# State-space scan with the output products of two heads issued together, one in each half of the array's columns, and a fourth decay matrix

## The chip, the cores and the metric

The kernel runs on one core of a Trainium2 chip, as one launch. The metric is the device time of that core in microseconds (us). TensorE is written PE in the profile (PEld its weight loads), VectorE DVE, ScalarE ACT, and SP the queue that issues the DMAs.

## The reference

The program computes, in float32, a two-layer transformer block on 256 tokens and 256 context tokens and then, on 16 + 256 tokens, one layer that joins a state-space scan with a short convolution and ends in a mixture of experts. The change lies in the scan. Its core in the reference is this, for 16 heads of 64 channels in 4 groups, in chunks of 128 tokens:

```python
seg = A_cum[..., :, None] - A_cum[..., None, :]
Lmat = jnp.exp(jnp.where(causal, seg, -jnp.inf)).astype(dtype)
CB = jnp.einsum('bcqgn,bckgn->bcgqk', Cc, Bc)
y_diag = jnp.einsum('bcgqk,bcgrqk,bckgrp->bcqgrp', CB, Lmat, xdt)
...
y_off = jnp.einsum('bcqgn,bcgrpn,bcgrq->bcqgrp', Cc, prev, decay_out)
return (y_diag + y_off).reshape(b, Lp, SSD_HEADS, SSD_HEADDIM)
```

## The kernel before

The kernel holds activations with features on the partitions and tokens along the free axis (272 here: a chunk of 16, two of 128). It does not carry a state from chunk to chunk. For each head it builds the whole causal matrix of decay times C.B over all pairs of chunks, and multiplies it with the head's inputs. The matrix of a head is 656 columns wide in SBUF: columns 0 to 272 belong to the 16 source tokens of the first chunk and use 16 partitions, 272 to 528 to the second chunk's 128 source tokens, 528 to 656 to the third's. It is called `EE`, and before the change there are three of them, used in turn by h % 3.

The work of a head h is spread over three engines:

- TensorE broadcasts the running sums of the decays (`pe_head_decay`, L2154, three float32 products, six instructions in the trace, since the trace shows two for each float32 product).
- VectorE adds a bias and clips (L2184 to L2186), ScalarE takes six exponentials (L2167 to L2173), VectorE multiplies with C.B (L2190, L2191).
- TensorE forms the output (`pe_head_out`, L2201, L2202, L2203): 64 channels of `XD` times the matrix, in three products of 272, 256 and 128 columns that add up in one PSUM bank. An even head writes partitions 0 to 63 of the bank, an odd one 64 to 127, so two heads share a bank. After the odd head VectorE adds the skip term and gates (L2216, L2219).

The scan is interleaved with a projection, the second half of `win`: 24 output tiles of 24 float32r matmuls each (L486 to L488 in `mm3`, three matmuls for a product, since both operands are held as a high and a low part). The weights of two tiles arrive in one DMA, ScalarE makes the high part (L461), VectorE the low part (L471). After tile f TensorE runs step f - 1 of the scan (`pe_scan`); VectorE and ScalarE run the same steps in their own programs. Step f = 5 + i does the decay part of head i and the output part of head i - 2. The short convolution lies between them: every third step VectorE computes a tile of it (L2027 to L2039), ScalarE squares it (L2017), and TensorE adds the sums of its squares (`pe_sc_sum`, L2046, 16 columns of the array). After every odd head from the second pair on, TensorE adds the squares of the pair before (L2230, 4 columns).

At step 22 stands `pe_sc_norm` for six convolution tiles. A spread (L2068) brings the inverse root of a tile's two groups to 64 partitions each, two products of 272 columns with 16 rows in the two halves of the array's columns. VectorE scales the tile (L2081), ScalarE copies its high part (L2076), VectorE subtracts the low part (L2084). The outputs of head 15 stand behind these spreads on TensorE. Then follows the output projection `wout`. In its first block of 36 matmuls each k waits for a tile's low part, and behind the block stand the last sum L2046 and the spreads of the last two tiles, which wait for a second square root (L2055, ScalarE) and reciprocal (L2060, VectorE). That reciprocal is called the second inverse below.

What sets the order are the programs of the engines, written out by hand. Each engine executes in order, and waits for counted marks of the others (`at`, `up`). PSUM has eight banks, handed out in turn: `bank` waits until the bank that was given back longest ago is free.

The program has other matmuls that use only some of the array's columns. L533 multiplies a modulation weight block with 32 columns, four products of 512 columns in the four 32-column strips, each with all 128 rows and another block of weights as moving data.

## Time and profile before

| | before |
|---|---|
| runs, us | 1783.9 median of three (1780.74 to 1784.62) |
| the profiled execution's own time | 1783.91 us |
| its span | 1782.1 us |
| PE busy | 1695.4 us (95%) |
| PEld busy | 1358.6 us (76%) |
| DVE busy | 1034.1 us (58%) |
| ACT busy | 832.7 us (47%) |
| mean granted TensorE clock | 0.977 of full |
| chain that ended last | PE 85%, DVE 7%, ACT 4% |

The profile is of one execution. Its span goes from the first to the last instruction, its own time also holds the start and the end. Busy time of an engine is the union of its instructions' times. The chain that ended last is followed back from the last instruction, at each step to what released it. A timeline row gives start, duration, engine, line and form, and in brackets how long the engine had been idle and what ended it. The clock is the share that the chip granted TensorE, 1.00 being 2.4 GHz and 0.50 being 1.2 GHz.

### The profile page before, as it was taken

How to read it: one execution, taken by the hardware profiler on the slowest of the kernel's cores; microseconds unless marked ns; L12 is line 12 of the kernel's file. 1: busy time of each engine (PE TensorE's matmuls, PEld its weight loads, DVE VectorE, ACT ScalarE, POOL GpSimd, SP SyncE). 2: the span in 40 equal slices, each digit the busy share in tenths (PEclk: the TensorE clock that was granted, in tenths of full speed). 3: DMA queues.
4: the chain of work that ended last, by engine and by line, in shares of the span. 5: the costliest groups of instructions: out<-in, count | busy, mean ns of one | idle time of the engine just before them, and what ended most of it. 6: DMA issues, size and time to landing. Idle time of an engine off the chain costs nothing.

```text
span 1782.1 us, 25094 instructions
## 1 busy us (share of the span) xinstructions
PE 1695.4 (95%) x10390; PEld 1358.6 (76%) x10390; DVE 1034.1 (58%) x1497; ACT 832.7 (47%) x1194; POOL 0.9 (0%) x5
## 2 busy tenths in 40 slices
PE   5989989999999999998898999999999999999996
PEld 2745667777877787898588999899876968777875
DVE  2235655544334444535756566647666558888885
ACT  3334552633223322523746454554444347766764
POOL 0000000000000000000000000000000000000000
PEclk7999999999999999999999999999998999999998
DMA  9311533344334424233024454344222419989982
GB/s 375 112 52 67 202 112 120 116 154 164 130 124 175 178 78 170 87 115 119 1 72 142 163 204 160 118 167 160 95 95 71 142 45 380 339 334 342 353 329 99
DMA packets 42678, 287.76 MB, mean 161 GB/s; under 512 B 4784, under 2 KB 5936, under 8 KB 11200
## 3 DMA queue, kind: packets, MB, share of 16 engines
q1 hardware_dynamic: 42384, 285.97, 44.0%
q8 instruction: 85, 1.39, 0.3%
q14 instruction: 33, 0.27, 0.0%
q10 hardware_dynamic: 144, 0.06, 0.0%
q0 software_dynamic: 32, 0.07, 0.0%
HBM read 285.03 MB, written 1.05 MB: 161 GB/s over the span
## 4 chain that ended last, share of the span: by engine, by line
PE 85%; DVE 7%; ACT 4%; issue 2%; DMA 1%; DVEq 0%; SPq 0%; ACTq 0%
PE ps L486 17%; PE ps L487 16%; PE ps L488 16%; PE ps L2670 5%; DVE WL L471 3%; PE ps L2640 2%; PE ps L2644 2%; PE ps L533 2%; PE ps L2641 2%; PE ps L1356 1%; PE ps L1454 1%; PE ps L1425 1%; DMA ring<-wts 1%; PE ps L511 1%; PE ps L613 1%
## 5 line engine op out<-in xcount | busy, mean ns | idle before, releaser
L486 PE MATMUL ps<-HH,WH 128*128 128x512 f32 (+2 forms) x1488 | 495.8, 333 | 17.4 <-DVE WL L471 10.2
L471 DVE TENSOR_TENSOR WL<-ring,WH 128x2048 fp32r<-128x2048 f32 (+2 forms) x191 | 413.5, 2171 | 164.4 <-ACT WH L461 164.1
L488 PE MATMUL ps<-HH,WL 128*128 128x512 f32 (+2 forms) x1488 | 484.8, 326 | 0.0
L487 PE MATMUL ps<-HL,WH 128*128 128x512 f32 (+2 forms) x1488 | 484.2, 325 | 0.0
L461 ACT ACTIVATE WH<-ring 128x2048 fp32r<-128x2048 f32 (+2 forms) x191 | 346.7, 1817 | 206.4 <-DMA ring<-wts 77.9
L486 PEld LDWEIGHTS ps<-HH,WH 128*128 128x128 f32 x1488 | 284.8, 191 | 68.3 <-issue 32.7
L488 PEld LDWEIGHTS ps<-HH,WL 128*128 128x128 f32 x1488 | 284.9, 191 | 21.8
L487 PEld LDWEIGHTS ps<-HL,WH 128*128 128x128 f32 x1488 | 285.4, 192 | 20.8 <-issue 0.5
L486 PE MATMUL ps<-parts,WH 128*128 128x512 f32 (+1 forms) x352 | 119.7, 340 | 0.0
L487 PE MATMUL ps<-parts,WH 128*128 128x512 f32 (+1 forms) x352 | 118.4, 336 | 0.0
L488 PE MATMUL ps<-parts,WL 128*128 128x512 f32 (+1 forms) x352 | 118.3, 336 | 0.0
L2640 PE MATMUL ps<-WH,HH 128*128 128x512 f32 x256 | 102.4, 400 | 6.6 <-DVE WL L471 6.6
L829 DVE SCALAR_TENSOR_TENSOR X<-ps,modv,X 128x256 f32<-128x256 f32 x72 | 32.4, 481 | 124.5 <-PE ps L488 124.5
L2644 PE MATMUL ps<-WH,HL 128*128 128x512 f32 x256 | 100.0, 391 | 0.0
L2641 PE MATMUL ps<-WL,HH 128*128 128x512 f32 x256 | 99.8, 390 | 0.0
L471 DVE TENSOR_TENSOR WL<-arena,WH 128x2048 fp32r<-128x2048 f32 x38 | 86.4, 2287 | 3.9 <-ACT WH L461 3.7
L461 ACT ACTIVATE WH<-arena 128x2048 fp32r<-128x2048 f32 x38 | 72.8, 1919 | 31.4 <-PE ps L2644 17.2
L2670 PE MATMUL ps<-WH,parts 128*128 128x512 f32 x256 | 72.9, 396 | 2.7 <-DVE parts L2751 1.5
L486 PEld LDWEIGHTS ps<-parts,WH 128*128 128x128 f32 x352 | 66.8, 190 | 9.0 <-issue 1.8
L488 PEld LDWEIGHTS ps<-parts,WL 128*128 128x128 f32 x352 | 66.8, 190 | 6.9
L487 PEld LDWEIGHTS ps<-parts,WH 128*128 128x128 f32 x352 | 66.8, 190 | 6.6
L533 PE MATMUL ps<-ring,scond 128*32 128x512 f32 x384 | 55.7, 659 | 14.5 <-DMA ring<-wts 8.1
(350 smaller groups left out, 2213.9 us busy)
## 6 DMA issues: line engine op xcount, KB each, us to landing
ring<-wts SPq DMA_DIRECT2D x206, 1024.0 KB, 5.0
arena<-wts SPq DMA_DIRECT2D x38, 1024.0 KB, 6.5
ring<-wts SPq DMA_DIRECT2D x32, 704.0 KB, 4.1
X<-xin SPq DMA_DIRECT2D x4, 512.0 KB, 9.2
cst<-csts SPq DMA_DIRECT2D x1, 1373.0 KB, 15.3
ring<-wts SPq DMA_DIRECT2D x3, 384.0 KB, 2.9
out<-arena SPq DMA_DIRECT2D x2, 512.0 KB, 2.9
ring<-wts SPq DMA_DIRECT2D x1, 640.0 KB, 3.5
```

What stands on the lines that cost most here:

```text
L461: e.activation(split_parts(i)[0], raw(i), ACT.Copy).then_inc(*up("high", i))
L471: e.tensor_tensor(lo, raw(i), hi.bitcast(F32), ALU.subtract).then_inc(*up("low", i))
L486: e.matmul(o, w[0][:, cols], x[0], start=k == 0, stop=False)
L487: e.matmul(o, w[0][:, cols], x[1], start=False, stop=False)
L488: return e.matmul(o, w[1][:, cols], x[0], start=False, stop=k == nk - 1)
L511: e.matmul(o[1][m], v[0][:, 256 * k + 128 * m:256 * k + 128 * m + 128], at_k(x, k)[h], start=k == h == 0, stop=False)
L533: t = e.matmul(ps[32 * j:32 * j + 32, b, :], scond[:, 2 * k:2 * k + 32], w[:, 512 * j:512 * j + 512], start=k == 0, stop=k == 7)
L829: t = e.scalar_tensor_tensor(out=X[:, j, a:z], in0=B("out", key, j)[:, a:z], scalar=modv[l][:, gt + j, s:s + 1], in1=X[:, j, a:z], op0=ALU ...
L2640: e.matmul(ps[:, b, :], XG[0][:, k, g], w[0][:, s], start=k == 0, stop=False)
L2641: e.matmul(ps[:, b, :], XG[0][:, k, g], w[1][:, s], start=False, stop=False)
L2644: t = e.matmul(ps[:, b, :], XG[1][:, k, g], w[0][:, s], start=False, stop=k == 7)
L2670: t = e.matmul(ps[:, bs[n], :], HTE[p][:, z, hs], w[q][:, s], start=first and p == q == 0, stop=last and p == 1)
```

## The change

`pe_head_out` does nothing for an even head. For an odd head it takes the bank, waits for the decay matrices of both heads of the pair, and issues their six products in alternation: the first chunk's for the even head and for the odd one, then the second chunk's, then the third's. The heads' shapes and numbers are unchanged, and so is the number of products. Since an even head's matrix is now read a step later, there are four matrices in place of three. The fourth lies in `cst` from the table `r128` on, over tables that only the attention stages read. ScalarE and VectorE wait before they write a matrix for the output of head h - 4 in place of h - 3. Lines behind the change move by 2 to 8: L2154 becomes L2156, L2184 to L2186 and L2190, L2191 move by 2, L2068 and L2081 become L2070 and L2083, L2203's successor is L2210 for all three products, L2216 and L2230 become L2224 and L2238.

```diff
--- before.py
+++ after.py
@@ -1793,7 +1793,9 @@
         YP = parts(16, NT)
         top[0] = 0
         ZS, XC, YC, XD = area(8, NT), area(16, NT), area(8, NT), area(3, 1024)
-        CBm, EE = area(4, 656), area(3, 656)
+        CBm, EE3 = area(4, 656), area(3, 656)
+        late = cat["r128"][0]
+        EE = [EE3[:, z, :] for z in range(3)] + [cst[:, late:late + 656]]
         dtr, dab, dtl, dtt, dA, aex = (area(48) for _ in range(6))
         bias6 = area(96)
         spare = XF[:, 8 * NT:]
@@ -2159,55 +2161,61 @@
             return lambda i, n: bias6[0:n, 16 * i + h:16 * i + h + 1]
 
         def act_head_decay(e, h):
-            z, y = h % 3, h % 2
+            EZ, y = EE[h % 4], h % 2
             b, bc = B("head", h), head_bias(h)
             e.wait_ge(*at("head_mixed.near", h))
-            if h >= 3:
-                e.wait_ge(*at("head_out", h - 3))
-            e.activation(EE[0:16, z, 0:16], SG2[0:16, y, 0:16], ACT.Exp).then_inc(*up("head_exp.meta", h))
-            e.activation(EE[0:16, z, 16:144], b[0:16, 16:144], ACT.Exp, bias=bc(3, 16), scale=1.0)
-            e.activation(EE[0:16, z, 144:272], b[0:16, 144:272], ACT.Exp, bias=bc(4, 16), scale=1.0)
-            e.activation(EE[:, z, 400:528], b[:, 144:272], ACT.Exp, bias=bc(5, 128),
+            if h >= 4:
+                e.wait_ge(*at("head_out", h - 4))
+            e.activation(EZ[0:16, 0:16], SG2[0:16, y, 0:16], ACT.Exp).then_inc(*up("head_exp.meta", h))
+            e.activation(EZ[0:16, 16:144], b[0:16, 16:144], ACT.Exp, bias=bc(3, 16), scale=1.0)
+            e.activation(EZ[0:16, 144:272], b[0:16, 144:272], ACT.Exp, bias=bc(4, 16), scale=1.0)
+            e.activation(EZ[:, 400:528], b[:, 144:272], ACT.Exp, bias=bc(5, 128),
                          scale=1.0).then_inc(*up("head_exp.far", h))
-            e.activation(EE[:, z, 272:400], EE[:, z, 272:400], ACT.Exp)
-            e.activation(EE[:, z, 528:656], EE[:, z, 528:656], ACT.Exp).then_inc(*up("head_exp", h))
+            e.activation(EZ[:, 272:400], EZ[:, 272:400], ACT.Exp)
+            e.activation(EZ[:, 528:656], EZ[:, 528:656], ACT.Exp).then_inc(*up("head_exp", h))
 
         def dve_head_decay(e, h):
-            z, y = h % 3, h % 2
+            EZ, y = EE[h % 4], h % 2
             b, bc = B("head", h), head_bias(h)
             e.wait_ge(*at("decay_bias"))
             e.wait_ge(*at("head", h))
             if h >= 2:
                 e.wait_ge(*at("head_exp.meta", h - 2))
-            if h >= 3:
-                e.wait_ge(*at("head_out", h - 3))
+            if h >= 4:
+                e.wait_ge(*at("head_out", h - 4))
             e.tensor_scalar(SG2[0:16, y, 0:16], b[0:16, 0:16], bc(0, 16), 0.0, ALU.add, ALU.min)
-            e.tensor_scalar(EE[:, z, 272:400], b[:, 16:144], bc(1, 128), 0.0, ALU.add, ALU.min)
-            e.tensor_scalar(EE[:, z, 528:656], b[:, 144:272], bc(2, 128), 0.0, ALU.add,
+            e.tensor_scalar(EZ[:, 272:400], b[:, 16:144], bc(1, 128), 0.0, ALU.add, ALU.min)
+            e.tensor_scalar(EZ[:, 528:656], b[:, 144:272], bc(2, 128), 0.0, ALU.add,
                             ALU.min).then_inc(*up("head_mixed.near", h))
             e.wait_ge(*at("head_exp", h))
             e.wait_ge(*at("cb_masked", h // 4, 1))
-            e.tensor_tensor(EE[0:16, z, 0:272], EE[0:16, z, 0:272], CBm[0:16, h // 4, 0:272], ALU.mult)
-            e.tensor_tensor(EE[:, z, 272:656], EE[:, z, 272:656], CBm[:, h // 4, 272:656],
+            e.tensor_tensor(EZ[0:16, 0:272], EZ[0:16, 0:272], CBm[0:16, h // 4, 0:272], ALU.mult)
+            e.tensor_tensor(EZ[:, 272:656], EZ[:, 272:656], CBm[:, h // 4, 272:656],
                             ALU.mult).then_inc(*up("head_mixed", h))
 
         def pe_head_out(e, h):
-            z, r, x = h % 3, 64 * (h % 2), h // 2
-            b = banks.of["y", x] if h % 2 else bank(e, "y", x)
-            hc = slice(64 * h, 64 * h + 64)
-            e.wait_ge(*at("head_mixed", h))
-            if h == 0:
+
+            if h % 2 == 0:
+                return
+            x = h // 2
+            b = bank(e, "y", x)
+            pair = (h - 1, h)
+            for i in pair:
+                e.wait_ge(*at("head_mixed", i))
+            if h == 1:
                 e.wait_ge(*at("xd", 2, 1))
-            e.matmul(ps[r:r + 64, b, 0:272], XD[0:16, 0, hc], EE[0:16, z, 0:272], start=True, stop=False)
-            e.matmul(ps[r:r + 64, b, 16:272], XD[:, 1, hc], EE[:, z, 272:528], start=False, stop=False)
-            e.matmul(ps[r:r + 64, b, 144:272], XD[:, 2, hc], EE[:, z, 528:656], start=False,
-                     stop=True).then_inc(*up("head_out", h))
-            if h % 2:
-                banks.give(b, "y_gated.skip", x)
-                if x == 0:
-                    bank(e, "group_sums")
-                else:
-                    pe_group_sum(e, x - 1)
+            for c, o, a, n in ((0, 0, 0, 272), (1, 16, 272, 256), (2, 144, 528, 128)):
+                for i in pair:
+                    r = 64 * (i % 2)
+                    t = e.matmul(ps[r:r + 64, b, o:o + n], XD[0:TLEN[c], c, 64 * i:64 * i + 64],
+                                 EE[i % 4][0:TLEN[c], a:a + n], start=c == 0, stop=c == 2)
+                    if c == 2:
+                        t.then_inc(*up("head_out", i))
+            banks.give(b, "y_gated.skip", x)
+            if x == 0:
+                bank(e, "group_sums")
+            else:
+                pe_group_sum(e, x - 1)
 
         def dve_head_out(e, h):
             if h % 2:
```

On TensorE, step 9 of the scan before (head 4's broadcasts, head 2's outputs) and the start of the next tile:

```order
L2154 MATMUL ps<-cst,arena 128x16
L2154 MATMUL ps<-cst,arena 128x128 x2
L2201 MATMUL ps<-arena 64x272
L2202 MATMUL ps<-arena 64x256
L2203 MATMUL ps<-arena 64x128
L486 MATMUL ps<-HH,WH 128x272
```

The same step with the change:

```order
L2156 MATMUL ps<-cst,arena 128x16
L2156 MATMUL ps<-cst,arena 128x128 x2
L486 MATMUL ps<-HH,WH 128x272
L487 MATMUL ps<-HL,WH 128x272
L488 MATMUL ps<-HH,WL 128x272
```

Nothing stands between the broadcasts and the tile any more. On TensorE, step 10 before (head 5's broadcasts, head 3's outputs, the sum of the squares of the first pair, a sum of the short convolution):

```order
L2154 MATMUL ps<-cst,arena 128x16
L2154 MATMUL ps<-cst,arena 128x128 x2
L2201 MATMUL ps<-arena 64x272
L2202 MATMUL ps<-arena 64x256
L2203 MATMUL ps<-arena 64x128
L2230 MATMUL ps<-arena,cst 4x272
L2046 MATMUL ps<-X,cst 16x272
```

The same step with the change, where the rows that read `cst` are those of head 3, whose matrix is the fourth:

```order
L2156 MATMUL ps<-cst,arena 128x16
L2156 MATMUL ps<-cst,arena 128x128 x2
L2210 MATMUL ps<-arena 64x272
L2210 MATMUL ps<-cst,arena 64x272
L2210 MATMUL ps<-arena 64x256
L2210 MATMUL ps<-cst,arena 64x256
L2210 MATMUL ps<-arena 64x128
L2210 MATMUL ps<-cst,arena 64x128
L2238 MATMUL ps<-arena,cst 4x272
L2048 MATMUL ps<-X,cst 16x272
```

Head 2's three products have moved here, each ahead of head 3's of the same chunk. The order on the other engines is unchanged.

## Rows read from the trace of the kernel before

**Rows 1.** Windows, head steps: stretch, its us, busy us by engine, clock, DMA, GB/s.

```profile
1260.10:1356.60 96.50, 96.50 (x619) 76.06 (x618) 62.88 (x131) 47.88 (x127) 0.00 (x0) 1.00 0.25 88
```

**Rows 2.** Chain of waits, steps f = 5 to 10; start us, us, what.

```profile
1260.15 0.96 PE ps L2154 x6
...
1264.14 0.96 PE ps L2154 x6
...
1279.82 0.96 PE ps L2154 x6
1280.79 0.60 PE ps L2201 x2
1281.38 0.58 PE ps L2202 x2
1281.96 0.22 PE ps L2203 x2
...
1285.40 0.96 PE ps L2154 x6
```

**Rows 3.** Timeline, TensorE column-tiled products; start us, us, engine, line, form, count, [idle before].

```profile
173.52 0.16 PEld L533 LDWEIGHTS ps<-ring,scond 128*32 128x32 f32 x8 [0.17 <-issue]
173.52 1.06 PE L533 MATMUL ps<-ring,scond 128*32 128x512 f32 x8
...
1360.16 1.11 PE L2201 MATMUL ps<-arena 16*64 16x272 f32 x2
1361.20 1.12 PE L2202 MATMUL ps<-arena 128*64 128x256 f32 x2
...
1374.62 2.08 PE L2068 MATMUL ps<-X,cst 16*64 16x272 f32 x8 [4.02 <-DVE X L2060]
1376.62 1.07 PE L2230 MATMUL ps<-arena,cst 128*4 128x272 f32 x2
```

**Rows 4.** Timeline of VectorE, its waits in the head steps.

```profile
1284.24 0.43 DVE L2190 TENSOR_TENSOR arena<-arena 16x272 f32<-16x272 f32 x1 [1.43 <-ACT arena L2173]
...
1286.46 0.22 DVE L2184 TENSOR_SCALAR X<-ps,arena 16x16 f32<-16x16 f32 x1 [1.32 <-issue]
...
1298.62 0.22 DVE L2184 TENSOR_SCALAR X<-ps,arena 16x16 f32<-16x16 f32 x1 [0.74 <-issue]
...
1310.87 0.22 DVE L2184 TENSOR_SCALAR X<-ps,arena 16x16 f32<-16x16 f32 x1 [0.78 <-PE ps L2154]
...
1322.56 0.22 DVE L2184 TENSOR_SCALAR X<-ps,arena 16x16 f32<-16x16 f32 x1 [2.50 <-issue]
...
1334.71 0.22 DVE L2184 TENSOR_SCALAR X<-ps,arena 16x16 f32<-16x16 f32 x1 [0.73 <-issue]
```

**Rows 5.** Head 12: its last VectorE product, and its output products on TensorE.

```profile
1333.44 0.54 DVE L2191 TENSOR_TENSOR arena<-arena 128x384 f32<-128x384 f32 x1
...
1340.74 0.60 PE ps L2201 x2
```

**Rows 6.** Timeline of VectorE, last weight split, first spread, second inverse.

```profile
1353.75 2.29 DVE L471 TENSOR_TENSOR WL<-ring,WH 128x2048 fp32r<-128x2048 f32 x1
1357.30 0.50 DVE L2081 SCALAR_TENSOR_TENSOR arena<-arena,vec,ps 128x272 f32<-128x272 f32 x1 [1.26 <-PE ps L2068]
...
1372.72 1.84 DVE L2060 RECIPROCAL X<-X 16x272 f32<-16x272 f32 x1 [1.89 <-ACT X L2055]
```

**Rows 7.** Windows: two stretches at the lower TensorE clock, and one after.

```profile
1359.10:1365.80 6.70, 6.48 (x18) 2.94 (x19) 4.22 (x11) 2.15 (x5) 0.00 (x0) 0.50 0.15 64
...
1372.80:1386.20 13.40, 11.58 (x41) 8.15 (x42) 8.94 (x13) 3.67 (x6) 0.00 (x0) 0.50 0.16 65
1386.40:1400.00 13.60, 13.60 (x101) 12.58 (x100) 7.90 (x13) 3.31 (x6) 0.00 (x0) 1.00 0.43 151
```

**Rows 8.** Windows of the stages after the scan.

```profile
1378.00:1440.00 62.00, 61.96 (x461) 54.33 (x461) 35.67 (x51) 21.87 (x28) 0.00 (x0) 0.93 0.29 103
...
1500.00:1560.00 60.00, 58.45 (x269) 47.15 (x268) 49.06 (x30) 42.42 (x32) 0.00 (x0) 1.00 0.90 340
```

## The prediction, made before the changed kernel was run

> **What bounds the kernel now.** I read the windows view over the sixteen head steps first. TensorE is busy for all 96.5 us of it, VectorE for 62.9 and ScalarE for 47.9 [rows 1]. So there each microsecond of TensorE work is on the path of the stage. The chain of waits shows what it holds: per head three broadcast sums (L2154), then the output products of the head two before (L2201, L2202, L2203) at 0.60, 0.58 and 0.22 us, which is 1.40 [rows 2]. A step without output products lasts 1264.14 - 1260.15 = 3.99 us and one with them 1285.40 - 1279.82 = 5.58 [rows 2]. The products therefore cost 1.59 us a step, 0.19 more than their own time: what the array loses when it turns from 128-column tiles to 64-column ones and back.
>
> Second, I read VectorE's timeline for idle time that TensorE ends. Its wait for ScalarE's exponentials, 1.43 us before L2190, belongs to a head's own chain and stays. Five waits before L2184 end with the broadcast sums: 1.32 + 0.74 + 0.78 + 2.50 + 0.73 = 6.07 us [rows 4]. One more comes at the end, 1.26 us before the first spread is used (L2081) [rows 6]. That is 7.33 us in all. This number matters because of what comes behind it. From 1357.30 to 1374.62 the work runs as a ladder on VectorE and ScalarE: six times L2081, L2076 and L2084, then the last gate, the last short-convolution tile, a weight split, a square root with its table load, and the reciprocal L2060 [rows 6]. TensorE waits 4.02 us for that reciprocal [rows 3]. So what reaches the rest of the kernel is not what TensorE saves, but how much earlier VectorE gets to L2081.
>
> **The change, part by part.** *Pairing.* Per pair six products are issued in alternation over the two column halves, where before 2 x 3 were issued in two different steps. Whether two halves run at once is the question. No row has 128 rows on 64-column tiles side by side with different moving data, so I bound it by its neighbours. L533 has 128 rows, four 32-column strips and a different moving block for each: its eight passes over 512 columns take 1.06 us, and all eight weight loads are done in 0.16 [rows 3]. L2068 has 16 rows and two 64-column halves. At the lower clock, two pairs of heads' spreads, eight passes of 272 columns, take 1376.62 - 1374.62 = 2.00 us, 1.00 a pair. At the same clock one single head's L2201, two passes of the same width, takes 1361.20 - 1360.16 = 1.04 [rows 3]. The second half is free there. I take free. The other bound is no overlap at all.
>
> With free overlap a pair costs what one head costs, and the even head's products vanish from its step. There are eight even heads. In five of their steps (heads 2, 4, 8, 10, 14) nothing narrow is left and the full 1.59 goes. In three (0, 6, 12) the 16-column sum L2046 still follows, so the turn of the tile shape stays and 1.40 goes. TensorE's saving is 5 x 1.59 + 3 x 1.40 = **12.1 us**. Without overlap only the turns go, 5 x 0.19 = 1.0 us.
>
> A rule of the Trainium skill speaks against the free half: "TensorE: Matmul & The Clock Gate", Part 3, says that a weight load overlaps a matmul in flight only where the row groups differ. Both halves here use all rows, so by it nothing would overlap and the sum would be the 1.0 us. The trace disagrees: L533's strips share all 128 rows, and its loads still ran within 0.16 us.
>
> *Four decay matrices.* No instruction is added. The fourth lies over constants that only the attention stages read. The wait for head_out(h - 3) becomes one for head_out(h - 4). For an even h that output now leaves TensorE in the same step as output h - 3 did before, for an odd h a step earlier than it did, so VectorE meets no later wait. An even head's matrix is held a step longer, and the fourth matrix covers that. Cost 0.
>
> *Deferred even output.* The pair waits for the odd head's last product, as the odd head did before. Head 12's product was ready at 1333.98, its output started at 1340.74 [rows 5], so 6.8 us of slack lie there. TensorE can come at most 12.1 - 7.3 = 4.8 us closer to VectorE, so no wait comes in its place inside the steps. The y bank is taken a step later, which frees a bank sooner. Cost 0.
>
> *What reaches VectorE.* Before the wait of 1.32 us (head 5) TensorE has saved heads 0 and 2, 2.99 us. Before those of heads 7, 9, 11 and 13 it has saved 4.58, 5.98, 7.57 and 9.16, against 2.06, 2.84, 5.34 and 6.07 of waits to that point [rows 2, 4]. At L2081 it is 12.1 against 7.33. TensorE is ahead each time, so all six waits go and nothing more. The remaining 4.8 us become idle time on TensorE inside the six spreads, because the later ones and the products behind them need PSUM banks that ScalarE and VectorE (L2081) free.
>
> *Behind the scan.* TensorE is 100% and 97% busy in two windows behind [rows 8], and the weight loads follow the splits. I take a pure shift. Before, the clock was at its lower level in two stretches, 1359.1 to 1365.8 and 1372.8 to 1386.2 [rows 7]. Both follow TensorE's thin or missing work around the two spreads, and I take both as they are. Costs: the first dip may last through the first block of the out projection. Busy time there is 13.60 us / 101 matmuls = 0.135 us each at the full clock [rows 7], so its 36 matmuls would lose at most 4.9, less a slack of at most the 4.02 us wait: 0.9 to 4.9 if it happens. The second dip could end earlier. It costs at most half of 1386.2 - 1374.6 = 11.6 us, so 5.8 is the most that could be won and I count 1 to 2 either way.
>
> **The sum.** The profiled execution took 1783.91 us (span 1782.1), and the median of three runs is 1783.9, so nothing is to be corrected between them. 1783.9 - 7.3 = **1776.6 us**, 0.4% faster. About 0.2%, 3.6 us, is what a measurement of this kernel can tell from no change, so "faster" means under 1780.3.
>
> **The rivals.**
> 1. *The clock takes some back.* TensorE will idle longer before the fifth spread, about 4.8 us more. If the first dip covers the block behind it (0.9 to 4.9) and the second ends later (1 to 2), 3.5 us go and the time is 1780.1. For it: the lower clock follows idle stretches here. Against: it came back by 1365.8, soon after dense work began at 1364.8.
> 2. *The whole 12.1 us arrive*, if VectorE can catch up as well: 1771.8. Against: after its six waits VectorE has the 1.43 us waits on ScalarE and its own work, none of which the change touches.
> 3. *The halves run one after the other*, by the page's rule above. TensorE saves 1.0 us and the time is 1782.9: the change would not do what it says.
> 4. *Slower.* The halves do not overlap, and each alternation between them pays the turn of the tile shape. Place: 6 turns in each of 8 pairs, 48. Price: 0.19 us each [rows 2], 9.1 us, less 1.0: +8.1 on a TensorE that bounds the steps, 1792.0. It decides from 0.02 us a turn for any loss, from 0.10 for one over 0.2%. Against: L2068 alternates halves in just this way and pays none [rows 3].
>
> **How the numbers follow.** Forecast 0.74, with 1775 to 1778.5 as its own range. Rival 1 0.10, rival 2 0.05, rival 3 0.07, rival 4 0.04. Faster: the forecast, rival 2 and half of rival 1, which lies at the edge: 0.84. Same: rival 3 and the other half of rival 1: 0.12. Slower: 0.04. The range leaves out rivals 3 and 4 and the far end of rival 2, and goes from 1772.5 (a second dip that ends early, or part of rival 2) to 1780.5 (rival 1).
>
> **What would show it.** In the changed kernel the products at L2210 should start in twos, so that a pair's six take about 1.4 us. An even head's step should be about 4.0 us, the five waits of VectorE before L2184's successor should be gone, and TensorE should wait some 5 us within L2070, the new place of L2068. The second reciprocal should end about 7.3 us earlier, at 1367.2, with the stages behind unchanged in length. It is wrong if a pair takes near 2.8 us (rivals 3 and 4), if L2083 starts over 9 us earlier (rival 2), or if the two stretches at the lower clock change by more than 3 us.

## The result, and the profile after

The changed kernel takes 1774.85 us (median of five runs, 1773.07 to 1776.6), against 1783.3 us (five runs, 1780.74 to 1784.62) for the kernel before on the same chip: a ratio of 0.9958 with a 95% interval of 0.9946 to 0.9969. By the medians that is 8.45 us less, by the ratio 7.5 (5.5 to 9.6), where 7.3 were forecast. The runs don't tell these apart. The profiled execution took 1774.6 us, 9.31 less than the one before.

The page of the changed kernel starts so:

```profile
span 1772.8 us, 25093 instructions
...
PE 1683.5 (95%) x10390; PEld 1351.8 (76%) x10390; DVE 1033.3 (58%) x1497; ACT 833.2 (47%) x1194; POOL 0.9 (0%) x5
```

TensorE is busy 11.9 us less (1695.4 before). VectorE and ScalarE do the work they did.

The windows view of the changed kernel over its head steps, its two stretches at the lower clock and one behind them (columns as in [rows 1]):

```profile
1261.18:1345.64 84.46, 84.46 (x612) 70.68 (x611) 58.36 (x126) 44.55 (x121) 0.00 (x0) 1.00 0.29 100
1350.40:1357.20 6.80, 6.32 (x24) 2.38 (x24) 4.33 (x12) 2.58 (x7) 0.00 (x0) 0.50 0.44 154
1367.50:1374.30 6.80, 6.59 (x23) 3.85 (x24) 4.10 (x8) 1.23 (x3) 0.00 (x0) 0.50 0.08 31
1374.40:1388.00 13.60, 13.60 (x101) 12.59 (x100) 9.36 (x14) 5.35 (x6) 0.00 (x0) 1.00 0.25 83
```

The head steps last 84.5 us instead of 96.5 [rows 1]. The first stretch at the lower clock is as long as before, the second 6.8 us instead of some 13.7 [rows 7]. In the last window the same 101 matmuls fill the same 13.60 us.

TensorE's timeline, changed kernel: an even head's step, a pair's step in the middle of the scan, and the spreads.

```profile
1261.16 1.03 PE L2156 MATMUL ps<-cst,arena 16*128 16x16 f32 x6
...
1321.62 1.03 PE L2156 MATMUL ps<-cst,arena 16*128 16x16 f32 x6
...
1325.60 1.03 PE L2156 MATMUL ps<-cst,arena 16*128 16x16 f32 x6
1326.56 0.44 PE L2210 MATMUL ps<-arena 16*64 16x272 f32 x1
1326.57 0.44 PE L2210 MATMUL ps<-cst,arena 16*64 16x272 f32 x1
1326.84 0.39 PE L2210 MATMUL ps<-arena 16*64 16x272 f32 x1
1326.85 0.39 PE L2210 MATMUL ps<-cst,arena 16*64 16x272 f32 x1
1327.16 0.43 PE L2210 MATMUL ps<-arena 128*64 128x256 f32 x1
1327.17 0.43 PE L2210 MATMUL ps<-cst,arena 128*64 128x256 f32 x1
...
1327.96 0.62 PE L2238 MATMUL ps<-arena,cst 128*4 128x272 f32 x2
...
1337.43 1.48 PE L2210 MATMUL ps<-arena 16*64 16x272 f32 x12
1338.84 0.62 PE L2238 MATMUL ps<-arena,cst 128*4 128x272 f32 x2
...
1345.64 1.59 PE L2070 MATMUL ps<-X,cst 16*64 16x272 f32 x12
1347.86 0.67 PE L2070 MATMUL ps<-X,cst 16*64 16x272 f32 x4 [0.63 <-DVE arena L2224]
1350.88 2.08 PE L2070 MATMUL ps<-X,cst 16*64 16x272 f32 x8 [2.35 <-ACT X L2016]
```

The products start in twos, 10 ns apart, one in each half of the columns. From a pair's first product to the instruction behind its last one it takes 1.40 us (1327.96 - 1326.56), and 1.41 in the other row; one head took 1.40 in the same measure [rows 2]. An even head's step lasts 1325.60 - 1321.62 = 3.98 us. And within the six spreads TensorE, which waited for nothing there before, now waits 0.63 and 2.35 us, for banks that VectorE and ScalarE have to free.

The weight loads of one such pair of products, changed kernel (PEld):

```profile
1327.16 0.13 PEld L2210 LDWEIGHTS ps<-arena 128*64 128x64 f32 x1 [0.41 <-issue]
1327.17 0.13 PEld L2210 LDWEIGHTS ps<-cst,arena 128*64 128x64 f32 x1
1327.21 0.14 PEld L2210 LDWEIGHTS ps<-arena 128*64 128x64 f32 x1
1327.22 0.14 PEld L2210 LDWEIGHTS ps<-cst,arena 128*64 128x64 f32 x1
```

Four loads with all 128 rows start within 0.06 us, while the matmuls that started at 1327.16 and 1327.17 are under way. By themselves they don't show that the halves run at once; the matmuls' own starts do.

VectorE's timeline, changed kernel: head 5, then the last split, the first use of the spread and the second inverse.

```profile
1280.95 2.29 DVE L471 TENSOR_TENSOR WL<-ring,WH 128x2048 fp32r<-128x2048 f32 x1
1283.15 0.22 DVE L2186 TENSOR_SCALAR X<-ps,arena 16x16 f32<-16x16 f32 x1
1286.14 0.22 DVE L2186 TENSOR_SCALAR X<-ps,arena 16x16 f32<-16x16 f32 x1
...
1348.20 2.28 DVE L471 TENSOR_TENSOR WL<-ring,WH 128x2048 fp32r<-128x2048 f32 x1
1350.40 0.49 DVE L2083 SCALAR_TENSOR_TENSOR arena<-arena,vec,ps 128x272 f32<-128x272 f32 x1
...
1365.82 1.84 DVE L2062 RECIPROCAL X<-X 16x272 f32<-16x272 f32 x1 [1.89 <-ACT X L2057]
```

No L2186 has idle time before it, where L2184 had it five times [rows 4], and the 1.26 us before the first use of the spread [rows 6] are gone.

Below, three lengths are read from each trace, since executions start the scan up to 5.4 us apart (1257.2 to 1262.6 us). The **lead** goes from the first broadcast sum to VectorE's first use of the spread. The **ladder** goes from there to the end of the second inverse. The **rest** goes from the start of the second spreads to the end. For the two profiles:

| | before | after | difference |
|---|---|---|---|
| first broadcast sum | 1260.08 | 1261.16 | +1.08 |
| lead | 97.22 | 89.24 | -7.98 |
| ladder (the second spreads start 0.05 us behind it) | 17.27 | 17.26 | -0.01 |
| rest | 407.5 | 405.1 | -2.4 |

These add up to the 9.3 us between the two profiled executions. The first row lies ahead of anything the change touches.

### The profile page after: what moved, and what is told of

Its sections match the earlier page's. It is cut to its first block, busy times and chain, and to the rows that moved or that the text cites. A ratio compares the mean times of both kernels' runs of the same rounds, so it can differ in the third digit from the quotient of the medians.

```text
span 1772.8 us, 25093 instructions
## 1 busy us (share of the span) xinstructions
PE 1683.5 (95%) x10390; PEld 1351.8 (76%) x10390; DVE 1033.3 (58%) x1497; ACT 833.2 (47%) x1194; POOL 0.9 (0%) x5
## 3 DMA queue, kind: packets, MB, share of 16 engines
q8 instruction: 85, 1.39, 0.3%
## 4 chain that ended last, share of the span: by engine, by line
PE 84%; DVE 8%; ACT 5%; issue 2%; DMA 1%; DVEq 0%; SPq 0%; ACTq 0%
PE ps L486 17%; PE ps L488 16%; PE ps L487 16%; PE ps L2678 5%; DVE WL L471 3%; PE ps L2648 2%; PE ps L2652 2%; PE ps L533 2%; PE ps L2649 2%; PE ps L1356 1%; PE ps L1454 1%; PE ps L1425 1%; DMA ring<-wts 1%; PE ps L511 1%; PE ps L613 1%
## 5 line engine op out<-in xcount | busy, mean ns | idle before, releaser
L486 PE MATMUL ps<-HH,WH 128*128 128x512 f32 (+2 forms) x1488 | 494.3, 332 | 17.9 <-DVE WL L471 10.2
L471 DVE TENSOR_TENSOR WL<-ring,WH 128x2048 fp32r<-128x2048 f32 (+2 forms) x191 | 413.4, 2170 | 164.1 <-ACT WH L461 163.8
L471 DVE TENSOR_TENSOR WL<-arena,WH 128x2048 fp32r<-128x2048 f32 x38 | 86.4, 2287 | 4.0 <-ACT WH L461 3.9
L533 PE MATMUL ps<-ring,scond 128*32 128x512 f32 x384 | 56.1, 663 | 13.8 <-DMA ring<-wts 7.4
```

Of the source, the lines that this page charges most:

```text
L471: e.tensor_tensor(lo, raw(i), hi.bitcast(F32), ALU.subtract).then_inc(*up("low", i))
L486: e.matmul(o, w[0][:, cols], x[0], start=k == 0, stop=False)
L533: t = e.matmul(ps[32 * j:32 * j + 32, b, :], scond[:, 2 * k:2 * k + 32], w[:, 512 * j:512 * j + 512], start=k == 0, stop=k == 7)
```

## The experiments

"Before" stood at 1782.4 to 1782.9 us (medians of 7 to 20 runs) beside these kernels. The short names in brackets are those that the expectations use. TensorE's lead is the distance from the first broadcast sum to the first spread; the last column has the lengths of the stretches at the lower clock around the two spreads.

| kernel | median us (range, n) | ratio to before, 95% | TensorE's lead | lead | ladder | rest | lower clock |
|---|---|---|---|---|---|---|---|
| before | 1783.3 (1780.74-1784.62, 5) | 1 | 96.49 | 97.22 | 17.27 | 407.5 | 6.8, 13.7 |
| after | 1774.85 (1773.07-1776.6, 5) | 0.9958 (0.9946-0.9969) | 84.48 | 89.24 | 17.26 | 405.1 | 6.8, 6.8 |
| four matrices only (e1) | 1783.18 (1780.48-1784.92, 10) | 1.0004 (0.9995-1.0014) | 96.49 | 97.21 | 17.28 | 406.9 | 3.4, 10.2 |
| one after the other (e2) | 1779.75 (1776.51-1783.07, 10) | 0.9984 (0.9974-0.9994) | 94.11 | 95.09 | 17.27 | 405.6 | 6.8, 6.8 |
| before, filled (e5) | 1787.2 (1784.27-1791.16, 10) | 1.0028 (1.0018-1.0037) | 101.04 | 101.76 | 17.27 | 405.4 | 3.4, 6.8 |
| after, filled (e3) | 1776.32 (1774.82-1779.28, 5) | 0.9966 (0.9952-0.998) | 89.02 | 89.74 | 17.28 | 408.6 | 3.4, 10.2 |
| less VectorE work (e4) | 1772.51 (1772.1-1774.16, 4) | 0.9946 (0.9929-0.9962) | 84.48 | 86.48 | 17.27 | 404.9 | 3.4, 6.8 |
| after, again (e8) | 1773.65 (1772.49-1774.44, 4) | 0.9948 (0.9931-0.9964) | 84.48 | 89.21 | 17.26 | 404.9 | 6.8, 6.8 |
| shorter ladder (e6) | 1770.56 (1765.36-1774.34, 4) | 0.9929 (0.9904-0.9954) | 84.48 | 89.27 | 14.27 | 404.3 | 6.8, 3.4 |
| the same again (e11) | 1772.56 (1768.19-1774.62, 6) | 0.994 (0.9926-0.9955) | 84.48 | 89.23 | 14.53 | 405.9 | 6.8, 6.8 |
| root earlier too (e7) | 1773.06 (1768.59-1773.73, 4) | 0.9936 (0.992-0.9953) | 84.48 | 89.21 | 15.35 | 406.6 | 10.2, 10.2 |
| last sum earlier too (e9) | 1766.13 (1764.17-1766.75, 4) | 0.9905 (0.989-0.992) | 84.48 | 89.18 | 12.73 | 403.1 | 10.2, none |
| the same again (e13) | 1766.38 (1763.7-1768.18, 4) | 0.9906 (0.9889-0.9923) | 84.48 | 89.24 | 12.42 | 403.1 | 6.8, none |
| that, filled (e10) | 1769.76 (1768.07-1770.41, 6) | 0.9927 (0.9915-0.9939) | 87.66 | 89.20 | 12.36 | 404.2 | none, 3.4 |

The first question was which part of the change does it, and whether VectorE's idle time is the measure of the gain.

### Four matrices only

The order of the output products is that of before; only the matrices are four, and the waits go to head h - 4.

```diff
-            z, r, x = h % 3, 64 * (h % 2), h // 2
+            z, r, x = h % 4, 64 * (h % 2), h // 2
...
-            e.matmul(ps[r:r + 64, b, 0:272], XD[0:16, 0, hc], EE[0:16, z, 0:272], start=True, stop=False)
+            e.matmul(ps[r:r + 64, b, 0:272], XD[0:16, 0, hc], EE[z][0:16, 0:272], start=True, stop=False)
```

> Kernel before with the fourth decay matrix alone: each head's three products stay in their own step. Theory (the gain is TensorE time from two halves at once, and the matrix only makes room for the deferred head): no gain, within 2 us of before, VectorE's five waits of 1.32, 0.74, 0.78, 2.50 and 0.73 us still there. Rival (a matrix more lets VectorE and ScalarE run ahead, and that brings part of the gain): 2 us or more faster.

Ratio 1.0004, and all of VectorE's waits stand as they were. Its timeline, four matrices only:

```profile
1283.58 0.22 DVE L2186 TENSOR_SCALAR X<-ps,arena 16x16 f32<-16x16 f32 x1 [1.32 <-issue]
...
1319.68 0.22 DVE L2186 TENSOR_SCALAR X<-ps,arena 16x16 f32<-16x16 f32 x1 [2.50 <-issue]
...
1354.42 0.50 DVE L2083 SCALAR_TENSOR_TENSOR arena<-arena,vec,ps 128x272 f32<-128x272 f32 x1 [1.27 <-PE ps L2070]
```

These are the 1.32 and 2.50 of [rows 4] and the 1.26 of [rows 6]. The fourth matrix is worth nothing by itself. The gain is in the pairing of the products.

### One after the other

The pair stands where the change puts it, but the even head's three products come first and then the odd head's.

```diff
-            for c, o, a, n in ((0, 0, 0, 272), (1, 16, 272, 256), (2, 144, 528, 128)):
-                for i in pair:
+            for i in pair:
+                for c, o, a, n in ((0, 0, 0, 272), (1, 16, 272, 256), (2, 144, 528, 128)):
```

> The changed kernel with the even head's three products ahead of the odd head's three, in place of alternation. Theory (alternation is what puts two halves side by side): the six products take near 2.8 us at the full clock against 1.4, TensorE saves only the turns of tile shape, 1.0 us, and the time is 1781 to 1784. Rival (the array overlaps the halves whatever the order, as it runs both in their own columns): six products in 1.4 to 1.6 us and 1774 to 1777, as the changed kernel.

TensorE's timeline, one after the other:

```profile
1286.31 1.03 PE L2156 MATMUL ps<-cst,arena 16*128 16x16 f32 x6
1287.27 1.46 PE L2210 MATMUL ps<-arena 16*64 16x272 f32 x6
1288.66 1.46 PE L2210 MATMUL ps<-cst,arena 16*64 16x272 f32 x6
1290.05 0.62 PE L2238 MATMUL ps<-arena,cst 128*4 128x272 f32 x2
```

Each head takes 1.39 us from start to start, 2.78 for the pair, although the two write to different halves of the columns. One pair of neighbours lies in different halves here too, the even head's last product (128 rows, 128 columns) and the odd head's first (16 rows, 272 columns), and it doesn't overlap: the even head takes 1.39 us to the start of the odd one, no less than a head by itself. So with the same twelve instructions the halves overlap in alternation and not in this order. Whether the alternating products must also agree in rows and width, as they do in the changed kernel, was not tested.

This kernel is also what rival 3 of the prediction described, and it shows an error in that rival's price. TensorE's lead is not 1.0 us shorter but 2.38. The pairing also takes head 14's products, 1.40 us, out of the step before the spreads and puts them behind the spreads with head 15's. With the turns' 1.0 that makes 2.4. VectorE's lead is 2.13 shorter, and the median 2.7 (0.9984, interval 0.9974 to 0.9994), 1.25 us under the range of 1781 to 1784 that was expected.

### Before, filled, and after, filled

Both get the same extra TensorE work: 20 matmuls of 512 columns into the bank of the first spread, just ahead of it. Nothing reads their result.

```diff
+                if x == 0:
+                    pe_warm(e, b, 20, HH)
                 for h in range(2):
```

> The kernel before with the same 20 extra matmuls (4.4 us) ahead of the first spread. Theory (there TensorE bounds the steps, VectorE waits for the first spread): the first spread is used 4.4 us later and the kernel is 3.5 to 4.5 us slower, 1786 to 1787, unless a clock that stays up behind the busy stretch gives 1 to 2 us back. Rival (the ladder behind hides TensorE work of this size in any kernel): within 1 us of before.

> The changed kernel with 20 extra matmuls of 512 columns (some 4.4 us, results overwritten) ahead of the first spread. Theory (VectorE bounds the steps now, TensorE has some 4 us of idle time in the spreads): 0 to 1 us slower than the changed kernel, or a little faster if the busy array keeps its clock; 1773 to 1776. Rival (TensorE's time is still the path, its saving arrives in full): 4.4 us slower, 1779.

The work is 101.04 - 96.49 = 4.55 us in the one and 89.02 - 84.48 = 4.54 in the other. VectorE's timeline of before, filled:

```profile
1354.22 2.28 DVE L471 TENSOR_TENSOR WL<-ring,WH 128x2048 fp32r<-128x2048 f32 x1
1362.32 0.50 DVE L2083 SCALAR_TENSOR_TENSOR arena<-arena,vec,ps 128x272 f32<-128x272 f32 x1 [5.81 <-PE ps L2070]
```

and of after, filled:

```profile
1344.63 2.29 DVE L471 TENSOR_TENSOR WL<-ring,WH 128x2048 fp32r<-128x2048 f32 x1
1347.33 0.50 DVE L2085 SCALAR_TENSOR_TENSOR arena<-arena,vec,ps 128x272 f32<-128x272 f32 x1 [0.41 <-PE ps L2072]
```

In the kernel before, VectorE waits 5.81 us instead of 1.26 and the lead grows by 4.54. In the changed one it waits 0.41 instead of nothing and the lead grows by 0.50. So 4.0 of the 4.5 us don't reach VectorE. TensorE's timeline of after, filled, at the start of the output block, shows what it meets there:

```profile
1354.81 0.36 PE L486 MATMUL ps<-HH,WH 128*128 128x272 f32 x1 [2.97 <-DVE arena L2085]
```

TensorE comes to this matmul early and waits until VectorE has scaled its sixth tile. It starts 8.2 us behind the first spread, with 2.97 us of idle time, where in the changed kernel it took 12.24 us, with 3.61 idle. Most of the difference is not idle time. Without the fill the clock was at its lower level for 6.8 us of this distance and the products in it took 8.6 us; with it all of them ran at 1.00 and took 5.2. So the room that TensorE has behind the first spread took in the fill, and the faster clock made part of that room. This pair of runs shows most directly that the path of this stage has moved from TensorE to VectorE. The medians say the same with more noise: +4.3 us for before (0.2 over the expected range), +1.5 to +2.7 for after against its two sets of runs. The rest of the profiled execution was 3.5 us longer here, with a second stretch at the lower clock of 10.2 us.

### Less VectorE work

The multiplication of the 16-partition part of each decay matrix with C.B is left out.

```diff
-            e.tensor_tensor(EZ[0:16, 0:272], EZ[0:16, 0:272], CBm[0:16, h // 4, 0:272], ALU.mult)
```

> The changed kernel without the product L2192 (L2190 before) of every head: the 16-partition part of the decay matrix is not multiplied with C.B, 16 instructions that add some 0.36 us each to VectorE's path, 5.8 us. Theory (VectorE bounds the steps, TensorE stands 4.1 us ahead of it at the first spread): the first spread is used 4 us earlier and the kernel is 4 us faster than the changed one, 1770 to 1772, then TensorE bounds again. Rival (TensorE bounds): no gain, 1774 to 1776.

VectorE's lead falls by 2.76 us with TensorE's unchanged at 84.48: VectorE's own work is on the path. That is less than the 16 x 0.36 = 5.8 us taken away, and less than the 4 us expected. VectorE's timeline, less VectorE work, shows where part of it went:

```profile
1302.52 0.22 DVE L2186 TENSOR_SCALAR X<-ps,arena 16x16 f32<-16x16 f32 x1 [0.24 <-issue]
...
1317.36 0.22 DVE L2186 TENSOR_SCALAR X<-ps,arena 16x16 f32<-16x16 f32 x1 [1.25 <-PE ps L2156]
...
1334.08 0.22 DVE L2186 TENSOR_SCALAR X<-ps,arena 16x16 f32<-16x16 f32 x1 [0.26 <-issue]
1338.05 1.84 DVE L2062 RECIPROCAL X<-X 16x272 f32<-16x272 f32 x1 [1.23 <-ACT X L2057]
```

It meets TensorE again in these three places (1.75 us of idle time) and waits 0.34 longer for the first square root (0.89 in the changed kernel). Set beside the changed kernel instruction by instruction, VectorE loses 2.4 us to TensorE, since two more waits, of 0.06 and 0.12 us, are too short for the view, and each wait also costs the small overlap that the next part describes under VectorE's waits. With the 0.34 for the root that leaves 3.0 us against the 2.76 measured; the last 0.2 stay open. The two engines lie close together inside the steps: a further gain on VectorE alone would soon be TensorE's again. The median, 1772.51, is 1.1 to 2.3 us under the two of the changed kernel, at the edge of what the runs can tell.

### The changed kernel again

No edit.

> The changed kernel again, as the measure for e6 and e7 on the same chip. Theory: 1774 to 1776, VectorE some 8 us earlier at the first spread than before, counted from the first head's broadcasts; the two stretches at the lower clock behind it vary between 3 and 14 us from execution to execution, which is the spread of the times.

1773.65 us, ratio 0.9948 (0.9931 to 0.9964). Lead and ladder repeat within 0.03 us. The median lies 0.35 us under the range.

### A shorter ladder

If all that is behind the scan hangs on the ladder, shortening it must pay. VectorE scaled a tile, waited 0.49 us for ScalarE's high part, and subtracted. Here it scales the next tile first.

```diff
+            def low(x):
+                e.wait_ge(*at("yc_high", x))
+                e.tensor_tensor(YP[1][:, 8 + x, :], YC[:, x, :], YP[0][:, 8 + x, :].bitcast(F32),
+                                ALU.subtract).then_inc(*up("yc_low", x))
+
...
-                e.wait_ge(*at("yc_high", x))
-                e.tensor_tensor(YP[1][:, 8 + x, :], YC[:, x, :], YP[0][:, 8 + x, :].bitcast(F32),
-                                ALU.subtract).then_inc(*up("yc_low", x))
+                if x > first:
+                    low(x - 1)
+            low(last)
```

> The changed kernel with VectorE's ladder of the spreads in another order: the next tile's L2083 stands ahead of the low part of the tile before, so VectorE does not wait 0.49 us for ScalarE's copy in each of six tiles. Theory (from the first spread to the second inverse VectorE is the path): the second inverse ends 2 to 3 us earlier and the kernel takes 1771.5 to 1773. Rival (TensorE's own work between the spreads, or the lower clock, sets that stretch): no gain, 1774 to 1776.

> e6 again, as the measure for e9 and e10 on the same chip and to narrow its interval. Theory: 1769 to 1772.5, 14.3 us from the first use of a spread to the end of the second inverse.

The ladder falls from 17.26 to 14.27 us, and to 14.53 in the second set. The medians are 1770.56 and 1772.56, which is 1.1 to 4.3 us under the changed kernel's two. The ladder's 3 us are there in the trace, but with a range of 9 us in the first set the size in the median isn't settled.

### The root earlier too

ScalarE's second square root is also put ahead of its first weight part of the output projection.

```diff
-            act_sc_root(e, 6, 7)
...
+                    if half and i == 0:
+                        act_sc_root(e, 6, 7)
```

> e6 and on ScalarE the second square root ahead of the weight copy L461 of 1.90 us that stood before it. Theory: VectorE's wait of 1.89 us for that root before the second inverse goes as well, the inverse ends another 1 to 1.9 us earlier, 1770 to 1771.5. Rival (the last sum, which TensorE issues behind the block of 36 matmuls, now comes last): under 0.5 us beyond e6.

The ladder is longer than without it, 15.35 us. ScalarE's timeline, root earlier too:

```profile
1358.33 1.28 ACT L2057 ACT_TABLE_LOAD   x1
1362.56 0.48 ACT L2057 ACTIVATE X<-ps,cst 16x272 f32<-16x272 f32 x1 [2.95 <-PE ps L2048]
```

The rival held. The root was ready 3 us before its input, the last sum (L2048), which stands behind the 36 matmuls of the first output block, partly at the lower clock here. One wait took the place of another, and the median is 0.5 to 2.5 us above the two of the shorter ladder.

### The last sum earlier too

So TensorE's last sum is moved into that block, behind 15 of its 36 matmuls.

```diff
-            pe_sc_sum(e, 7, 6, 7)
...
+                        if half and i == 0 and n == 5:
+                            pe_sc_sum(e, 7, 6, 7)
```

> e7 with the last tile's sum (L2048) moved on TensorE from behind the 36 matmuls of the first output block to behind 15 of them. Theory (in e7 ScalarE waited 2.95 us for that sum, which stood behind a block at the lower clock): the wait falls under 1 us, from the first use of a spread to the end of the second inverse it takes 13.0 to 13.6 us against 14.27 in e6 and 15.35 in e7, and the kernel takes 1768.5 to 1771. Rival (the wait has another cause, or the first block itself now holds TensorE up before the second spreads): 14 us or more there, 1771 to 1774.

> The kernel of the early sum again, unchanged, on another chip session, to see whether its time holds. If it does: the ladder from the first use of the spread to the second inverse 12.7 us again, and the median 1765 to 1768, with a ratio interval that ends below 0.994, under that of the changed kernel. If the 1766.1 came from executions that happened to have only one stretch at the lower clock: two such stretches in the trace, and a median of 1768 to 1771, 2 to 5 us higher.

ScalarE's timeline, last sum earlier too:

```profile
1357.35 1.28 ACT L2057 ACT_TABLE_LOAD   x1
1358.97 0.48 ACT L2057 ACTIVATE X<-ps,cst 16x272 f32<-16x272 f32 x1 [0.34 <-PE ps L2048]
```

The wait of 2.95 us is 0.34, the ladder 12.73 us (12.42 in the second set), less than the 13.0 to 13.6 expected. The time is 1766.13 us, and 1766.38 in the second set: ratios 0.9905 and 0.9906, intervals 0.989 to 0.992 and 0.9889 to 0.9923. The first median lies 2.4 us under its range, the second in its own. It is the fastest kernel here, 16 us under the kernel before and 7 to 9 under the changed one. The ladder has 4.5 to 4.8 of these, the rest 2.0 more. Both profiled executions show only one stretch at the lower clock around the spreads, of 10.2 and 6.8 us. None comes behind the second spreads, and the rest is 403.1 us in both, where the changed kernel had 405.1. TensorE no longer waits for the second inverse. Its timeline in the same kernel:

```profile
1361.68 1.13 PE L2070 MATMUL ps<-X,cst 16*64 16x272 f32 x8
```

No idle time stands before these spreads, where it was 4.02 us before [rows 3]; in the second set it is 0.19 us.

### That, filled

Fourteen matmuls are put ahead of the first spread as above, to see whether work in TensorE's idle time keeps the clock up.

```diff
+                if x == 0:
+                    pe_warm(e, b, 14, HH)
```

> e9 with 14 extra matmuls of 512 columns (3.1 us) ahead of the first spread, where TensorE waits anyway. Theory (they lie in its idle time, and a busy array keeps the full clock through head 15's products and the first output block): the first spread is used no later, the first stretch at the lower clock starts later or falls away, and the kernel is 0 to 1.5 us faster than e9. Rival (fill work costs what it does not gain, as the 1.5 us that e3 lost with 20): 0.5 to 2 us slower than e9.

It costs 3.6 us against the kernel without them (1769.76 against 1766.13), more than theory and rival had between them. VectorE starts the ladder no later (lead 89.20), and the clock stays up through the first spreads. But TensorE now meets its last sum early and waits. TensorE's timeline, that, filled:

```profile
1359.56 0.63 PE L2048 MATMUL ps<-X,cst 128*16 128x272 f32 x2 [2.26 <-ACT X L2019]
```

A stretch of 3.4 us at the lower clock follows at 1361.2, the second spreads start 0.45 us later after the lead (13.54 against 13.09), and the rest is 1.1 longer. That is 1.5 us of the 3.6. The two profiled executions also differ by 2.2 us in where the scan starts, before the added matmuls run, so how much of the remaining 2 belongs to the matmuls stays open.

## Why the prediction held

**The halves overlap.** Taken as free, and it is: 1.40 us from a pair's first product to the next instruction, 1.40 for one head before. TensorE's lead fell by 12.01 us (96.49 to 84.48), where 5 x 1.59 + 3 x 1.40 = 12.1 was worked out. Rivals 3 and 4 are out: the pair doesn't take 2.8 us, and 48 alternations cost no turn. By the rule on weight loads that the prediction took from the Trainium skill, "TensorE: Matmul & The Clock Gate", Part 3, nothing would have overlapped; the matmuls that start 10 ns apart on the same 128 rows speak against it. That weight loads run beside a matmul on the same rows is no evidence of its own: in "one after the other", where the heads don't overlap, a load starts at 1287.92 while the matmul from 1287.87 is under way, rows and half the same.

The prediction says that no row has 128 rows on 64-column tiles side by side with different moving data, and bounds the pair by L533 and L2068. But there are such rows. The attention stage of the kernel before has such products, two heads in alternation over the halves, each with its own weights and its own moving data. They stand just ahead of L533 in TensorE's timeline of before:

```profile
172.77 0.61 PE L1454 MATMUL ps<-arena 128*64 128x128 f32 x8
173.21 0.39 PE L1460 MATMUL ps<-cst,small 128*64 128x128 f32 x4
```

Eight passes of 128 columns, four in each half, take 0.44 us (173.21 - 172.77), so two passes side by side take 0.11. One head's L2203 took 0.22 for its two passes alone [rows 2]. The free half could have been read there, and its term needed no bound.

**Four matrices and the even output cost nothing.** The first was shown alone (ratio 1.0004). No new wait stands before L2192 or L2193 beyond the one for ScalarE's exponentials.

**VectorE's waits are the measure.** This was the step that set the number, and its mechanism held: all six waits went, TensorE's further 4 us did not arrive, and 4.5 us of TensorE work ahead of the first spread cost 0.50. The term was 7.33 us and measured 7.98. The waits were read from the idle time in brackets. But a VectorE instruction that doesn't wait starts before the end of the one ahead: L471 ends at 1280.95 + 2.29 = 1283.24, and L2186 starts at 1283.15. A wait therefore costs its idle time plus this overlap, 0.07 to 0.09 us here. Head 5 gained 1.40 for a bracket of 1.32, head 7 0.81 for 0.74, the first use of the spread 1.35 for 1.26. Over the six waits that is 0.45 of the 0.65 us by which the term was short. Another 0.16 came from heads 8, 10 and 14, where no bracket stood, 0.05 each.

**The ladder and behind it.** The ladder's length was said to stay, and did (17.27 and 17.26). The second inverse was forecast to end at 1367.2. It ends at 1365.82 + 1.84 = 1367.66, because this execution started its scan 1.08 us late; from the first broadcast sum it comes 7.99 us earlier. The time of 1776.6 lies 1.75 us above the median: 0.65 are this term, 0.6 the start from 1783.9 where five runs give 1783.3, and the other 0.5 is within what medians of one kernel differ by (1774.85 and 1773.65).

**TensorE's idle time.** Some 5 us within L2070 were expected; 0.63 + 2.35 = 2.98 stand there. The 4.0 by which TensorE's lead outran VectorE's show in the distance from the first spread to the first matmul of the output block: 12.24 us (1345.64 to 1357.88) where it was 8.20. Idle time makes 3.4 of it: 3.61 us, with 0.63 more before that matmul, which waits for L2083, in place of 0.24 in all before. The other 0.7 goes to products that ran at the lower clock for longer (6.8 us of this distance against 5.7).

**The clock.** Rival 1 lost. The first stretch kept its 6.8 us, and the second became shorter, not longer: 6.8 us, and the rest 2.4 shorter. But the prediction had named a change of either stretch by more than 3 us as a sign that it is wrong, and the second changed by 6.8. The sign was badly chosen. Over the fourteen profiles the stretches around these spreads last from nothing to 13.7 us, and they differ even where the instructions on TensorE are the same: 6.8 and 13.7 before, 3.4 and 10.2 with the fourth matrix alone. So the 2.4 us are not credited to the change; that the profiled execution gained them is luck. 7.98 alone would put the median at 1775.3, and 1774.85 and 1773.65 were measured.

Nor does the first stretch cost what rival 1 feared. TensorE's timeline, four matrices only, where no lower clock lies between the first spread (1353.70) and the output block:

```profile
1361.90 0.38 PE L486 MATMUL ps<-HH,WH 128*128 128x272 f32 x1 [2.65 <-DVE arena L2083]
```

That is 8.20 us behind the first spread, the same as in the kernel before, which had the lower clock for 5.7 of its 8.20 us. VectorE's scaling sets this distance; what the clock costs TensorE there is taken from a wait. Where the first stretch reaches into the output block it does cost: in "root earlier too" (10.2 us long) the block's 36 matmuls took 5.5 us to the last sum, in "shorter ladder" 4.7.

**Rival 2**, the whole 12.1 us, is out by the lead: 89.24 and not 85.2. **Rival 3** was mispriced. It left out that the pairing also defers head 14's products past the spreads. With the heads one after the other the time was 1779.75, not 1782.9.

## What to carry to other kernels

Two narrow float32 products can share the array's columns at no cost, with 16 rows and with all 128, and whether they do depends on their order in the program: here they did when they alternated one by one, in equal shapes, and not when each head's three came together. Before bounding such a cost, look through the whole trace for the same form; an earlier stage may have it. What the saving is worth is read from the idle time of the next engine, not from the saving: sum its waits up to the point that releases the following stage, and add to each the small overlap that back-to-back instructions have. Then look for what bounds that stage now. Here a chain of VectorE, ScalarE and one small TensorE sum behind the scan held 3 us in VectorE's order and 1.5 to 2 in the square root's wait, and the latter were won only once both the root and the sum it needs had been moved.

## What the runs showed of the hardware

- Of two column halves, six products in the order even, odd, even, odd, even, odd take 1.40 us to the start of the next instruction; in the order even, even, even, odd, odd, odd they take 2.78. The programs differ in nothing else.
- The lower clock around the two spreads lasted from nothing to 10.2 us at the first spreads and from nothing to 13.7 at the second. Between executions of one kernel, and between before and four matrices only, a stretch differed by up to 3.4 us.
- The rest of the program goes with the second stretch: 403.1 us in both profiles without one, 404.2 and 404.3 with 3.4 us, 404.9 to 405.9 with 6.8, 406.6 to 408.6 with 10.2, 407.5 with 13.7. Together with the start of the scan (1257.2 to 1262.6 us) these are the parts in which the profiled executions differ. Kernels whose lead and ladder repeat to 0.3 us spread by 2 to 9 us in time; that the same two parts make this spread is likely, but only one execution of each set has a trace.
- A stretch at the lower clock came at the second spreads in all eleven profiles in which TensorE had waited 2.4 to 4.5 us for the second inverse, and in neither of the two in which it had waited 0.2 us or less there and nowhere else in that block. In the fourteenth, the last one of the table, it had waited 2.26 us for the square a little earlier, and a stretch of 3.4 us came. That goes together; how long a stretch becomes I can't say from it.
